# Three rotary units of the sparse attention, moved from the product stage into the stage of the key search's scores

## The chip, the cores and the metric

The kernel runs on one core of one Trainium2 chip. The metric is the device time of one execution in microseconds, the median of several runs. The engines are TensorE (PE in the profile, PEld for its weight loads), VectorE (DVE), ScalarE (ACT), GpSimd (POOL) and SyncE (SP), which here only issues transfers.

## What is computed

Two models run one after the other: a block of linear-attention and recurrent mixers with a feed-forward part, and then two hybrid attention layers over 1024 positions of width 1024. The change is in the hybrid layers. What matters of one of them:

```python
h = jnp.einsum('bsd,de->bse', x, w_in)
(dq, dk, dv, sq, sk, sv, iq, ik, iw, fq, fk, fv, ff, gate) = split_columns(h)
...
sq = rope(sq.reshape(B, S, DSA_HEADS, DSA_DIM), pos)      # 4 heads of 64
sk = rope(sk, pos)                                        # one key head
iq = rope(iq.reshape(B, S, IDX_HEADS, IDX_DIM), pos)      # 8 heads of 64
ik = rope(ik, pos)
bo = dsa_attention(sq, sk, sv, iq, ik, iw * IDX_WEIGHT_SCALE, pos, topk)   # topk = 256
...
# in dsa_attention, per block of 128 queries
sc = jnp.einsum('bqhd,bsd->bqhs', qib, ki)
idx_score = jnp.einsum('bqhs,bqh->bqs', jax.nn.relu(sc), wib)
_, idx = lax.top_k(jnp.where(causal[None], idx_score, -jnp.inf), topk)
s = jnp.einsum('bqhd,bqkd->bhqk', qb, kk[idx]) * scale    # attention over the chosen keys
```

So `iq`, `ik` and `iw` are needed for the search of the keys, `sq` and `sk` only in the attention behind it.

## The kernel before, in words

A hybrid layer is the body of a loop of two turns. It is a sequence of stages; in each, all engines run their own list of instructions, held together by semaphores, and a stage begins when all have finished the one before. The matrix XT (the layer's input, transposed, and its rounding rest REST) lies in SBUF. Every product with it is made of three: high by high, high by rest, rest by high (`three_products`, lines 344 to 346). A rotary unit is 128 output features over 1024 positions: `unit_products` issues 2 halves of 512 positions x 8 slices of the contraction x 3 = 48 products of 128x512 into one pair of PSUM banks; there are four pairs. GpSimd splits the unit's weights into high part and rest (lines 451 and 453, or 2039 and 2041), VectorE multiplies the pair by cosine and by sine (lines 472 and 475, or 2121 and 2124), ScalarE's queue issues four transfers that swap the halves of 32 partitions (`turn_halves`, line 372), and VectorE adds the swapped half (line 466, or 2110).

The stages that matter, in this order:

1. The product stage ("pa", `product_stage`): eight rotary units, three for the sparse attention (SQ: four query heads in two, the key head in one) and five for the search (IQ), each in pair u % 4; then a wide product of 332 columns for all eight blocks of 128 positions, one PSUM bank each. Its first use of each pair waits for `scaled`, the second rotation product of the unit that lay there. ScalarE rounds SQ to SQ_high (line 439) and GpSimd subtracts it (line 457, SQ_rest).
2. The score stage (`index_stage`): 8 blocks of queries (t) times 8 heads (h), 64 rows j of 128 queries by 128(t+1) keys. TensorE computes two heads in a step, as products of 64 rows each in fp32 (line 1866), so there are 32 steps; ScalarE takes the relu (line 1878) into one of four slots, VectorE adds it, weighted, to the block's scores (line 1891), and per block takes the greatest (line 1898) and adds the causal mask (line 1899). PSUM pairs are used as j % 4. SyncE loads a few parameters for the attention.
3. The search stage (`search_stage`, "tk"): VectorE and ScalarE find the 256th greatest score of each query in 32 rounds of bisection (ScalarE counts in three blocks, line 1930, VectorE in three, line 1961, and joins them in lines 1965, 1966 and 1958), then VectorE writes the mask. Beside it TensorE computes 20 units (12 that ScalarE copies out, 8 rotary ones) and a wide product of 512 columns. From the 17th unit on it needs pairs that VectorE must free, which does so only behind the search.
4. The sparse attention, which reads SQ_high, SQ_rest and the mask, and the stages behind it.

Of the kernel before, what the change touches and what calls it, by code (L numbers as in the profile page):

```python
# [16 lines left out]
P = 128  # L17
# [357 lines left out]
def product_stage(kit, tag, XT, rest, items, ropes, rope, place, rot, partner, halves, wide):  # L375
# [9 lines left out]
    (products, taken, dve_own, scaled, rope_in, split, rounded, bank_done, wide_taken, high_done, low_done) = (  # L385
        kit.sem(f"{tag}_{n}") for n in ("products", "taken", "dve_own", "scaled", "rope_in", "split", "rounded",
                                        "bank_done", "wide_taken", "high_done", "low_done"))
    with ExitStack() as mem:
# [5 lines left out]
        with nc.Block() as block:  # L394
# [10 lines left out]
            def _(pe):  # L405
# [23 lines left out]
            def _(act):  # L429
                for n in range(U + 1):  # L430
# [14 lines left out]
            def _(pool):  # L445
                for i, (_, width) in enumerate(items):
# [1393 lines left out]
def index_stage(kit, IQ, VS, IS, AM, causal, prepare):  # L1840
# [3 lines left out]
    scored, bent, added, done, own_d = (kit.sem(f"ix_{n}") for n in ("scored", "bent", "added", "done", "own_d"))  # L1844
    H = 8
    SLOTS = 4
    with ExitStack() as mem:
        R = sbuf(nc, mem, "ix_R", [P, SLOTS, S])
        with nc.Block() as block:
            @block.sync  # L1850
            def _(sp):
                prepare.load(sp)

            @block.tensor
            def _(pe):
                for t in range(NT):
                    n = P * (t + 1)
                    for h in range(0, H, 2):
                        j = t * H + h
                        if j >= SLOTS:  # L1860
                            pe.wait_ge(bent, j + 1 - SLOTS + 1)
                        for c in range(0, n, HALF):
                            e = min(n, c + HALF)
                            for m in range(2):
# [3 lines left out]
                                if e == n:  # L1868
                                    last.then_inc(scored, 1)
# [1171 lines left out]
```

## Time and profile before

| | |
|---|---|
| median of 3 runs | 3120.19 us (3117.55 to 3122.45) |
| the profiled execution | 3115.68 us, its span 3114.0 us |
| mean granted TensorE clock | 0.964 |
| busy share: PE, PEld, DVE, ACT, POOL | 91%, 74%, 54%, 32%, 25% |
| product stage, score stage, search stage of layer 0, from us | 1356.8, 1473.8, 1539.2 |

Times in the views are microseconds from the span's start. Products are pipelined: each of 128x512 is recorded with 0.39 us, though one starts every 0.23 us, so a busy PE in a stretch says that it had work, not how much more would fit. A granted clock of 1 is 2.4 GHz, one of 0.5 is 1.2 GHz.

### The profile page before, as it was taken

How to read it: one execution, taken by the hardware profiler on the slowest of the kernel's cores; microseconds unless marked ns; L12 is line 12 of the kernel's file. 1: busy time of each engine (PE TensorE's matmuls, PEld its weight loads, DVE VectorE, ACT ScalarE, POOL GpSimd, SP SyncE). 2: the span in 40 equal slices, each digit the busy share in tenths (PEclk: the TensorE clock that was granted, in tenths of full speed). 3: DMA queues.
4: the chain of work that ended last, by engine and by line, in shares of the span. 5: the costliest groups of instructions: out<-in, count | busy, mean ns of one | idle time of the engine just before them, and what ended most of it. 6: DMA issues, size and time to landing. Idle time of an engine off the chain costs nothing. (4 is left out here: it accounts for less than half of the span.)

```text
span 3114.0 us, 39179 instructions
## 1 busy us (share of the span) xinstructions
PE 2840.1 (91%) x14936; PEld 2311.2 (74%) x14936; DVE 1677.7 (54%) x2806; ACT 983.8 (32%) x1911; POOL 791.7 (25%) x510
## 2 busy tenths in 40 slices
PE   6999888989999999989699889989897898999988
PEld 4768678778888888868388778777684686778767
DVE  5170476534223233333999545675446998265855
ACT  3150454220000000111564034563105560244751
POOL 2233103223233333323033261003130332340021
PEclk9999899999999999999999999999899999999999
DMA  3101002111111111131122420004320224300032
GB/s 113 35 34 49 1 1 99 48 41 38 51 58 38 50 59 48 55 122 47 41 89 89 139 92 1 1 13 165 131 64 3 96 87 123 141 1 1 1 135 95
DMA packets 83146, 194.07 MB, mean 62 GB/s; under 512 B 15488, under 2 KB 34448, under 8 KB 81936
## 3 DMA queue, kind: packets, MB, share of 16 engines
q1 hardware_dynamic: 71056, 153.78, 14.6%
q10 hardware_dynamic: 11904, 37.76, 3.9%
q8 instruction: 123, 2.02, 0.3%
q14 instruction: 63, 0.52, 0.1%
HBM read 141.18 MB, written 33.55 MB: 56 GB/s over the span
## 5 line engine op out<-in xcount | busy, mean ns | idle before, releaser
L344 PE MATMUL psum<-H,tk_W 128*128 128x512 f32 x640 | 250.9, 392 | 23.1 <-DVE OM L2124 22.9
L344 PE MATMUL psum<-H,ffn_W 128*128 128x512 f32 x672 | 262.9, 391 | 4.8 <-DVEq L1716 3.1
L346 PE MATMUL psum<-H,ffn_W 128*128 128x512 f32 x672 | 262.4, 390 | 0.0
L345 PE MATMUL psum<-H,ffn_W 128*128 128x512 f32 x672 | 262.4, 390 | 0.0
L345 PE MATMUL psum<-H,tk_W 128*128 128x512 f32 x640 | 250.3, 391 | 0.0
L346 PE MATMUL psum<-H,tk_W 128*128 128x512 f32 x640 | 250.0, 391 | 0.0
L1930 ACT ACTIVATE MB<-OM,tk_mid 128x384 bf16<-128x384 f32 (+2 forms) x192 | 157.2, 819 | 120.7 <-DVE tk_mid L1958 119.9
L1961 DVE TENSOR_SCALAR_CACHE_REDUCE MB<-OM,tk_mid 128x512 bf16<-128x512 f32 (+2 forms) x192 | 184.3, 1010 | 2.3
L1483 POOL CAST ffn_W<-ffn_W 128x1024 fp32r<-128x1024 f32 (+1 forms) x77 | 65.1, 845 | 471.4 <-PE psum L346 469.6
L2039 POOL CAST tk_W<-tk_W 128x1024 fp32r<-128x1024 f32 (+1 forms) x56 | 53.6, 958 | 512.1 <-PE psum L346 361.0
L1697 DVE TENSOR_SCALAR ffn_Y<-ffn_G,ffn_par 128x1024 f32<-128x1024 f32 x21 | 21.1, 1004 | 288.6 <-ACT ffn_G L1670 288.6
L1670 ACT ACTIVATE ffn_G<-psum 128x1024 f32<-128x1024 f32 x21 | 21.6, 1029 | 445.6 <-PE psum L346 445.6
L344 PEld LDWEIGHTS psum<-H,tk_W 128*128 128x128 f32 x640 | 121.0, 189 | 50.1 <-issue 23.7
L1485 POOL TENSOR_TENSOR ffn_W<-ffn_W,ffn_W 128x1024 fp32r<-128x1024 f32 (+1 forms) x77 | 152.6, 1982 | 6.2
L344 PEld LDWEIGHTS psum<-H,ffn_W 128*128 128x128 f32 x672 | 126.8, 189 | 32.3 <-POOLq L1556 3.5
L346 PEld LDWEIGHTS psum<-H,ffn_W 128*128 128x128 f32 x672 | 126.7, 189 | 26.7
L345 PEld LDWEIGHTS psum<-H,ffn_W 128*128 128x128 f32 x672 | 126.8, 189 | 26.1
L2715 POOL TENSOR_TENSOR fin_W_rest<-fin_W 128x2048 fp32r<-128x2048 f32 x4 | 22.4, 5604 | 462.8 <-ACT fin_W L2685 462.8
L346 PEld LDWEIGHTS psum<-H,tk_W 128*128 128x128 f32 x640 | 121.0, 189 | 25.4
L345 PEld LDWEIGHTS psum<-H,tk_W 128*128 128x128 f32 x640 | 121.0, 189 | 25.3
L344 PE MATMUL psum<-ffn_W,ffn_PR 128*128 128x512 f32 x336 | 131.1, 390 | 0.0
L346 PE MATMUL psum<-ffn_W,ffn_PR 128*128 128x512 f32 x336 | 130.8, 389 | 0.0
(442 smaller groups left out, 7219.7 us busy)
## 6 DMA issues: line engine op xcount, KB each, us to landing
tk_W<-in_w_feat SPq DMA_DIRECT2D x40, 512.0 KB, 3.6
ffn_W<-in_ffn_w_gate SPq DMA_DIRECT2D x21, 512.0 KB, 3.5
ffn_W<-in_ffn_w_val SPq DMA_DIRECT2D x21, 512.0 KB, 3.5
ffn_W<-in_ffn_w_down SPq DMA_DIRECT2D x42, 256.0 KB, 2.6
OM<-in_w_feat SPq DMA_DIRECT2D x16, 512.0 KB, 7.7
OM<-MB ACTq DMA_DIRECT2D x64, 128.0 KB, 2.4
GATE<-OM ACTq DMA_DIRECT2D x16, 512.0 KB, 2.9
OM<-OM ACTq DMA_DIRECT2D x64, 128.0 KB, 2.9
```

Of the source, the lines that this page charges most:

```text
L344: pe.matmul(out, a1, b1, start=start, stop=False)
L345: pe.matmul(out, a1, b2, start=False, stop=False)
L346: return pe.matmul(out, a2, b1, start=False, stop=stop)
L1483: pool.tensor_copy(w1, w).then_inc(self.rounded, 1)
L1485: pool.tensor_tensor(w2, w, w1.bitcast(FP32), ALU.subtract).then_inc(self.split, 1)
L1670: act.activation(G[:, j % 2, 2:2 + S], kit.pair(j % 2), ACT.Copy).then_inc(gate_out, 1)
L1697: own.then(dve.tensor_scalar(y, x[:, 2:2 + S], par[:, 2, j:j + 1], par[:, 3, j:j + 1], ALU.mult, ALU.add))
L1930: last = act.activation(self.MB[:, self.keys(t)], self.IS[:, self.keys(t)], ACT.Sign, scale=-1.0, bias=self.mid[:, 3 + n:4 + n], accum_out ...
L1961: own(dve.tensor_scalar(MB[:, self.keys(t)], IS[:, self.keys(t)], mid[:, n:n + 1], 0.0, ALU.is_lt, ALU.add, accum_out=self.cnt[:, n:n + 1]))
L2039: pool.tensor_copy(w1, w).then_inc(rounded, 1)
L2715: pool.tensor_tensor(w_part(W2, c, 0), w_part(W, c, 0), w_part(W1, c, 0).bitcast(FP32), ALU.subtract).then_inc(w_low_pool, 1)
```

## The change

The three units of the sparse attention leave the product stage, which keeps the five of the search. The score stage loads their weights and the rotation table, splits them on GpSimd, and computes their products in 48 chunks of three (one slice of the contraction of one half), a few behind each step, in proportion to the step's keys and none in the last four steps. The scores use three PSUM pairs; all three units use the fourth, one after the other. The number of chunks issued up to each step is `upto`. VectorE rotates unit u behind the second row of the step `last_step[u]`, in which the unit's last chunk is issued (steps 15, 22 and 27); ScalarE issues the swap four rows later, and VectorE adds the partner another four rows later. The rounding of SQ to its high part and rest goes to the search stage, both on GpSimd, behind its fourth to sixth weights.

```diff
-def product_stage(kit, tag, XT, rest, items, ropes, rope, place, rot, partner, halves, wide):
+def product_stage(kit, tag, XT, rest, items, ropes, rope, place, rot, partner, wide):
...
-                            pe.wait_ge(scaled, U - n_pairs + t // 2 + 1)
+                            pe.wait_ge(scaled, [u for u in range(U) if u % n_pairs == t // 2][-1] + 1)
...
-                    if 0 < n <= len(halves):
-                        plain, high, _ = halves[n - 1]
-                        act.wait_ge(taken, n)
-                        act.activation(high, plain, ACT.Copy).then_inc(high_done, 1)
...
-                    if 0 <= i - 3 < len(halves):
-                        plain, high, low = halves[i - 3]
-                        pool.wait_ge(high_done, i - 2)
-                        pool.tensor_tensor(low, plain, high.bitcast(FP32), ALU.subtract).then_inc(low_done, 1)
...
-def index_stage(kit, IQ, VS, IS, AM, causal, prepare):
+def index_stage(kit, IQ, VS, IS, AM, causal, prepare, XT, rest, items, ropes, rope, table, rot, partner):
...
+    H, SLOTS, PAIRS, PARTS, UNIT_PAIR, CHUNKS = 8, 4, 3, 2, 3, 2 * KT
+    U, STEPS = len(ropes), NT * H // 2
...
+    share = [j // 4 + 1 for j in range(STEPS - 4)]
+    upto = [min(CHUNKS * U, CHUNKS * U * sum(share[:j + 1]) // sum(share)) for j in range(STEPS)]
+    last_step = [[j for j in range(STEPS) if upto[j] >= CHUNKS * (u + 1)][0] for u in range(U)]
...
+                for i, (src, _) in enumerate(items):
+                    if i >= PARTS:
+                        sp.wait_ge(split, i - PARTS + 1)
+                    sp.dma_start(W[:, i % PARTS, :], src).then_inc(w_in[i % PARTS], 16)
+                    if i == 0:
+                        sp.dma_start(table, rope).then_inc(rope_in, 16)
                 prepare.load(sp)
...
+                for i in range(U):
+                    w, w1, w2 = (a[:, i % PARTS, :] for a in (W, W1, W2))
+                    pool.wait_ge(w_in[i % PARTS], 16 * (i // PARTS + 1))
+                    if i >= PARTS:
+                        pool.wait_ge(products, i - PARTS + 1)
+                    pool.tensor_copy(w1, w).then_inc(rounded, 1)
+                    pool.wait_ge(rounded, i + 1)
+                    pool.tensor_tensor(w2, w, w1.bitcast(FP32), ALU.subtract).then_inc(split, 1)
...
+                def chunk(n):
+                    u, c, k = n // CHUNKS, n % CHUNKS // KT, n % KT
+                    if n % CHUNKS == 0:
+                        pe.wait_ge(split, u + 1)
+                        if u:
+                            pe.wait_ge(scaled, u)
+                    w1, w2 = (a[:, u % PARTS, k * P:(k + 1) * P] for a in (W1, W2))
+                    at = slice(c * HALF, (c + 1) * HALF)
+                    last = three_products(pe, kit.pair(UNIT_PAIR)[:, at], w1, w2, XT[:, k, at], rest[:, k, at],
+                                          k == 0, k == KT - 1)
+                    if n % CHUNKS == CHUNKS - 1:
+                        last.then_inc(products, 1)
+
+                def scores(step):
+                    t, h = step * 2 // H, step * 2 % H
+                    n, j = P * (t + 1), 2 * step
+                    if j + 1 >= PAIRS:
+                        pe.wait_ge(bent, j + 1 - PAIRS + 1)
...
+                for step in range(STEPS):
+                    scores(step)
+                    for n in range(upto[step - 1] if step else 0, upto[step]):
+                        chunk(n)
...
+                    for u in range(U):
+                        if j == 2 * last_step[u] + 1 + SLOTS:
+                            act.wait_ge(scaled, u + 1)
+                            if u:
+                                act.wait_ge(turned, u)
+                            turn_halves(act, partner, rot, swapped)
...
+                def rotate(u):
+                    dst, scale = ropes[u]
+                    out = kit.pair(UNIT_PAIR)
+                    dve.wait_ge(products, u + 1)
+                    if u == 0:
+                        dve.wait_ge(rope_in, 16)
+                    else:
+                        dve.wait_ge(swapped, 64 * u)
+                    own(dve.scalar_tensor_tensor(dst, out, scale, cos, ALU.mult, ALU.mult))
+                    dve.scalar_tensor_tensor(rot, out, scale, sin, ALU.mult, ALU.mult).then_inc(scaled, 1)
+
+                def add_partner(u):
+                    dst = ropes[u][0]
+                    dve.wait_ge(swapped, 64 * (u + 1))
+                    own.wait()
+                    dve.tensor_tensor(dst, dst, partner, ALU.add).then_inc(turned, 1)
...
+                        for u in range(U):
+                            if j == 2 * last_step[u] + 1:
+                                rotate(u)
+                            if j == min(2 * last_step[u] + 1 + 2 * SLOTS, NT * H - 1):
+                                add_partner(u)
...
                     pool.tensor_tensor(w2, w, w1.bitcast(FP32), ALU.subtract).then_inc(split, 1)
+                    if 0 <= i - 3 < len(halves):
+                        plain, high, low = halves[i - 3]
+                        pool.tensor_copy(high, plain).then_inc(high_done, 1)
+                        pool.wait_ge(high_done, i - 2)
+                        pool.tensor_tensor(low, plain, high.bitcast(FP32), ALU.subtract).then_inc(low_done, 1)
...
-    items = [(w_feat[m], S) for m in range(8)]
-    items += rows_of(w_tok, 0, 332)
-    dst = [SQ[:, j, :] for j in range(3)] + [IQ[:, j, :] for j in range(5)]
-    ropes = [(dst[m], QK_SCALE if m < 2 else IDX_SCALE if 3 <= m < 7 else 1.0) for m in range(8)]
+    items = [(w_feat[3 + m], S) for m in range(5)] + rows_of(w_tok, 0, 332)
+    ropes = [(IQ[:, m, :], IDX_SCALE if m < 4 else 1.0) for m in range(5)]
...
-    index_stage(kit, IQ, VS, IS, AM, causal, prepare)
+    index_stage(kit, IQ, VS, IS, AM, causal, prepare, XT, REST, [(w_feat[m], S) for m in range(3)],
+                [(SQ[:, m, :], QK_SCALE if m < 2 else 1.0) for m in range(3)], rope, MB[:, 0:4 * S].bitcast(FP32),
+                flat[:, 5 * S:6 * S], flat[:, 6 * S:7 * S])
```

## Rows read from the trace of the kernel before

**Rows 1.** The page: busy time of each engine and its share.
```profile
PE 2840.1 (91%) x14936; PEld 2311.2 (74%) x14936; DVE 1677.7 (54%) x2806; ACT 983.8 (32%) x1911; POOL 791.7 (25%) x510
```

**Rows 2.** Stretches of layer 0: length, busy per engine, granted clock, DMA share, GB/s.
```profile
1356.80:1443.80 87.00, 86.97 (x384) 72.01 (x385) 29.28 (x20) 3.18 (x3) 32.60 (x19) 1.00 0.32 91
...
1473.80:1539.20 65.40, 40.32 (x192) 16.40 (x192) 57.70 (x80) 40.95 (x64) 0.00 (x0) 0.91 0.01 3
```

**Rows 3.** The page: products of the search stage, both layers.
```profile
L344 PE MATMUL psum<-H,tk_W 128*128 128x512 f32 x640 | 250.9, 392 | 23.1 <-DVE OM L2124 22.9
```

**Rows 4.** Timeline, VectorE, product stage: start, length, operation, idle before.
```profile
1379.00 1.23 DVE L472 SCALAR_TENSOR_TENSOR SQ<-psum,pa_table 128x1024 f32<-128x1024 f32 x1 [8.51 <-PE psum L346]
...
1381.27 2.38 DVE L466 TENSOR_TENSOR SQ<-SQ,OM 128x1024 f32<-128x1024 f32 x1
...
1444.21 1.22 DVE L472 SCALAR_TENSOR_TENSOR IQ<-psum,pa_table 128x1024 f32<-128x1024 f32 x1 [7.39 <-PE psum L346]
...
1446.48 1.22 DVE L466 TENSOR_TENSOR IQ<-IQ,OM 128x1024 f32<-128x1024 f32 x1
```

**Rows 5.** Timeline, all engines, start of the product stage.
```profile
1349.70 0.36 SPq L400 DMA_DIRECT2D OM<-in_w_feat  x1
...
1353.32 1.04 POOL L451 CAST pa_W<-OM 128x1024 fp32r<-128x1024 f32 x1 [57.76 <-DMA OM<-in_w_feat]
...
1356.83 0.50 PE L344 MATMUL psum<-H,pa_W 128*128 128x512 f32 x1 [0.96 <-POOL pa_W L453]
```

**Rows 6.** Timeline, PE, score stage: one step of 512 and one of 896 keys.
```profile
1488.59 1.13 PE L1866 MATMUL psum<-IQ 64*128 64x512 f32 x4 [0.42 <-ACT ix_R L1878]
...
1515.65 1.77 PE L1866 MATMUL psum<-IQ 64*128 64x512 f32 x8 [0.47 <-ACT ix_R L1878]
```

**Rows 7.** Timeline, PE, sparse attention: into and out of 64-row products.
```profile
1881.70 0.50 PE L2139 MATMUL psum<-SQ_high 64*128 64x512 f32 x2
...
1882.04 0.40 PE L2139 MATMUL psum<-SQ_rest,SQ_high 64*128 64x512 f32 x2
...
1882.85 0.34 PE L2139 MATMUL psum<-SQ_high,SQ_rest 64*128 64x384 f32 x2
...
1883.12 0.93 PE L2224 MATMUL psum<-MB,identb 128*128 128x512 bf16 x4
```

**Rows 8.** Timeline, VectorE, score stage.
```profile
1490.71 5.89 DVE L1891 SCALAR_TENSOR_TENSOR OM<-ix_R,VS,OM 128x512 f32<-128x512 f32 x7
...
1516.61 8.69 DVE L1891 SCALAR_TENSOR_TENSOR OM<-ix_R,VS,OM 128x896 f32<-128x896 f32 x7
...
1525.33 1.09 DVE L1898 TENSOR_REDUCE AM<-OM 128x1 f32<-128x896 f32 x1
...
1538.41 0.29 DVE L1899 TENSOR_TENSOR OM<-OM,CONST 128x128 f32<-128x128 f32 x1
```

**Rows 9.** Timeline, ScalarE and its queue, product and score stage.
```profile
1392.19 2.44 ACTq L372 DMA_DIRECT2D OM<-MB  x4
...
1516.60 0.92 ACT L1878 ACTIVATE ix_R<-psum 128x896 f32<-128x896 f32 x1 [0.99 <-DVE OM L1894]
```

**Rows 10.** Stretch of the search stage behind PE's wait, columns as in rows 2.
```profile
1732.00:1736.00 4.00, 4.00 (x11) 3.13 (x11) 1.90 (x3) 0.00 (x0) 0.00 (x0) 0.57 0.73 164
```

**Rows 11.** Timeline, VectorE, search stage: rounds of the bisection, and its end.
```profile
1541.76 0.22 DVE L1958 TENSOR_SCALAR tk_mid<-tk_lo,tk_steps 128x6 f32<-128x6 f32 x1
...
1576.80 0.17 DVE L1965 TENSOR_TENSOR tk_keep<-tk_cnt,tk_need 128x6 f32<-128x6 f32 x1
...
1580.52 0.17 DVE L1965 TENSOR_TENSOR tk_keep<-tk_cnt,tk_need 128x6 f32<-128x6 f32 x1
...
1580.73 2.37 DVE L1966 SCALAR_TENSOR_TENSOR tk_lo<-tk_keep,tk_steps,tk_lo 128x6 f32<-128x6 f32 x1
...
1684.52 0.17 DVE L1967 TENSOR_SCALAR tk_mid<-tk_lo 128x6 f32<-128x6 f32 x1
```

**Rows 12.** Timeline, GpSimd, search stage.
```profile
1580.69 2.39 POOL L2041 TENSOR_TENSOR tk_W<-tk_W 128x1024 fp32r<-128x1024 f32 x1
```

More of the change, by code:

```diff
@@ L384, in product_stage @@
     swapped = [kit.sem(f"{tag}_swapped{n}") for n in range(turns)]
-    (products, taken, dve_own, scaled, rope_in, split, rounded, bank_done, wide_taken, high_done, low_done) = (
+    products, taken, dve_own, scaled, rope_in, split, rounded, bank_done, wide_taken = (
         kit.sem(f"{tag}_{n}") for n in ("products", "taken", "dve_own", "scaled", "rope_in", "split", "rounded",
-                                        "bank_done", "wide_taken", "high_done", "low_done"))
+                                        "bank_done", "wide_taken"))
     with ExitStack() as mem:
@@ L1854, in _ @@
             @block.tensor
             def _(pe):
[L1856 to L1864, printed above, removed]
-                                rows = slice(64 * m, 64 * m + 64)
-                                last = pe.matmul(kit.pair((j + m) % SLOTS)[:, c:e], IQ[rows, h // 2, t * P:(t + 1) * P],
-                                                 IQ[rows, 4, c:e], start=True, stop=True)
-                                if e == n:
-                                    last.then_inc(scored, 1)
+                def chunk(n):
[10 more added lines that the diff above has]
+                        last.then_inc(products, 1)
@@ new lines, in scores @@
+                def scores(step):
[3 more added lines that the diff above has]
+                        pe.wait_ge(bent, j + 1 - PAIRS + 1)
+                    for c in range(0, n, HALF):
+                        e = min(n, c + HALF)
+                        for m in range(2):
+                            rows = slice(64 * m, 64 * m + 64)
+                            last = pe.matmul(kit.pair((j + m) % PAIRS)[:, c:e], IQ[rows, h // 2, t * P:(t + 1) * P],
+                                             IQ[rows, 4, c:e], start=True, stop=True)
+                            if e == n:
+                                last.then_inc(scored, 1)
@@ L1877, in _ @@
                         act.wait_ge(added, j - SLOTS + 1)
[L1878 removed]
+                    act.activation(R[:, j % SLOTS, 0:n], kit.pair(j % PAIRS)[:, 0:n], ACT.Relu).then_inc(bent, 1)
+                    for u in range(U):
[4 more added lines that the diff above has]
+                            turn_halves(act, partner, rot, swapped)
             @block.vector
@@ L1996, in select, with search_stage @@
             own.then(dve.tensor_scalar(MB[:, self.keys(t)], A[:, 0:n], 1.0, -NEG, ALU.subtract, ALU.mult))
-def search_stage(kit, XT, rest, items, topk, staged, partner, rot, fox, GATE, FQD, rope, DQD, DV):
+def search_stage(kit, XT, rest, items, topk, staged, partner, rot, halves, fox, GATE, FQD, rope, DQD, DV):
     nc = kit.nc
@@ L2893, in layer @@
         items += rows_of(w_tok, 332, 844)
-        search_stage(kit, XT, REST, items, topk, staged, slots_of(0, 2), slots_of(2, 4), [QK_SCALE] * 2 + [1.0] * 2, GATE, FQD, rope, DQD, DV)
+        search_stage(kit, XT, REST, items, topk, staged, slots_of(0, 2), slots_of(2, 4),
+                     [(SQ[:, m, :], SQ_high[:, m, :], SQ_rest[:, m, :]) for m in range(3)], [QK_SCALE] * 2 + [1.0] * 2, GATE, FQD, rope, DQD, DV)
     gates = ExitStack()
```

21 lines of the change are left out of this document (13 added, 8 removed).

## The prediction, made before the change was run

> **What bounds the kernel now.** I read the page's engine totals first: TensorE is busy 91% of the span [rows 1], so the question is where it is not. The stretches of layer 0 answer that [rows 2]. The eight rotary units of the product stage (1356.8 to 1443.8) keep PE at 86.97 of 87.00 us, and its wide half starts without a gap behind them: what leaves them is worth its full price. In the stage of the key search's scores, 1473.8 to 1539.2, PE is busy 40.32 of 65.40 us and VectorE 57.70. VectorE's rows there run without a gap, 5.89 us for seven accumulations of 512 keys, 8.69 us for seven of 896 [rows 8], and PE waits for ScalarE, which waits for VectorE: VectorE bounds this stage. Last comes the search stage behind it. Its page row [rows 3] has PE idle 22.9 us before the first product of a unit, released by VectorE's rotation at L2124: once in each layer, some 11.5 us, PE has all four PSUM pairs full while VectorE is still searching. So in that stage VectorE sets the time until PE starts again, and what delays VectorE before that point is paid in full.
>
> **Part 1: three units leave the product stage.** Rotations of consecutive units begin 10.87 us apart (1379.00 to 1444.21 is six units) [rows 4]; with 48 products a unit, one product is 0.2265 us. Three units: -32.6 us a layer. But the PSUM pair order changes. With five units the wide half's first tile lies in the pair of unit 4, the unit just finished, so PE waits for its rotation, whose two operations take 2.27 us by their starts [rows 4], 2.5 with the signals. Before, the last unit's pair was the fourth to be used, behind the products of six tiles, which hid it. Sum: -30.1 us a layer. ScalarE's three roundings and GpSimd's three remainders leave at no gain, as PE had no gap there.
>
> **Part 2: the same 144 products, in the score stage.** Count from PE's first score product (0).
>
> *Start.* The weights are loaded by this stage's own block. At the product stage's start, load issue to GpSimd's cast is 3.6 us (1349.70 to 1353.32) and the split is in use 3.5 us after that (1356.83) [rows 5]. So chunk 0, which stands behind step 2 (the whole-number rule gives 0, 0, 1 chunks up to steps 0, 1, 2), starts at 7.2. PE would otherwise be there after some 2 us, and all later scores stand behind the chunk: VectorE runs dry for some 5 us. The parameter loads now wait behind the third weight load; nobody needs them until the attention.
>
> *PE's chain from there to chunk 47.* 48 chunks of three products are 32.6 us. Scores: a step of 512 keys takes 1.13 us and one of 896 keys 1.77 [rows 6], so 0.213 us per 128 keys and 0.28 us of start and end; steps 3 to 27 have 109 such units, 23.2 us. New are the changes between 64-row fp32 pairs and 128-row products, which the stage does not show. The nearest rows are those of the sparse attention [rows 7]: entering 64-row products the second pair starts 0.34 us after the first, where a 512-column product takes 0.23; leaving them, the next starts 0.27 us after one of 384 columns, which takes 0.17. Add a late first start of some 0.1 us: I take 0.3 us a step for both changes, 24 steps, 7.2 us. Bounds: nothing, and 0.6 (the 0.28 exposed twice). The Trainium skill, "TensorEngine Tiling (Array Packing)", Key Properties, says that changing the tiling mode drains TensorE. By that rule each step also pays the drain, which makes the 0.3 more likely than nothing.
>
> *Two stalls.* All three units share one pair. Step 15 issues chunks 15 and 16 (floor of 48x40/112 is 17), step 22 chunks 31 and 32 (floor of 48x78/112 is 33): the first chunk of the next unit is in the same step as the last of the one before, and waits until that is rotated. VectorE must first take both rows of that step: after the scores, two relus (0.92 each at 896 keys [rows 9], say 0.65 at 512), an add of 0.84 (5.89/7 [rows 8]), then 2.3 of rotation, less the 0.7 of the chunk that runs meanwhile: 4.4 us with signals, about the same at 768 keys. Queued behind PE's wait are all further scores, so ScalarE and then VectorE run dry too. Twice: 8.8 us.
>
> Chain: 7.2 + 32.6 + 23.2 + 7.2 + 8.8 = 79.0 us.
>
> *Tail.* The last two rows before the third rotation come 2.1 us behind the chunks (two relus of 0.92, two adds of 1.24, beside 2.2 us of chunks), rotation 2.3, then what VectorE did from 1525.33 to 1538.70, 13.4 us [rows 8], and one add of the partner, 1.2 [rows 4]: 19.0. The stage: 98.0. The four swap issues on ScalarE's queue (2.44 us [rows 9]) fall thrice: in the last case four slots of relus lie ahead of VectorE, in the two others PE sets the pace and ScalarE catches up in a few rows. I take them at nothing; uncovered they cost 2.4 each.
>
> *Clock.* After its wait in the search stage, in which it did nothing, PE restarts at the 1.2 GHz level: the granted clock is 0.57 from 1732 to 1736 [rows 10], full before and soon after. PE's 5 us of idleness at the start of this stage should bring that level too: chunks run 4 us at half speed, 2.0 us. The boundary stalls are shorter and I add nothing for them; if each brings it, another 4.
>
> Stage after: 100.0, before 64.9 (1473.8 to 1538.7): +35.1 us a layer.
>
> *VectorE and GpSimd.* During GpSimd's subtraction of 2.39 us (1580.69) VectorE's L1966, an operation with two SBUF inputs on six columns, lasts 2.37 us [rows 11, 12]. The accumulations here have two SBUF inputs too, and three splits of 3.4 us run beside them: 3.4 of the first two while VectorE is dry anyway, the others while PE is the pace. I take nothing, at most 5. The Trainium skill, "SBUF — State Buffer", Who interferes with whom, says it as a rule: a VectorE instruction with two SBUF inputs and a GpSimd one that reads SBUF lock each other out for a whole instruction. By that rule up to 7 us of VectorE's time would go, most of it inside PE's waits; the trace agrees on the small tiles.
>
> **Part 3: the halves' rounding moves to GpSimd in the search stage.** Behind items 3, 4 and 5 GpSimd gets a cast and a subtraction more, 3.4 us each time, in VectorE's search. A round without GpSimd takes 3.72 us (1576.80 to 1580.52); 32 rounds last 142.7 us (1541.76 to 1684.52) [rows 11] where 119.0 would do: 23.7 us went with 14 splits (two at its start, then one every 10.9 us), 1.7 each. Three more: +5.1 us a layer, and PE's wait of rows 3 grows by it. Bounds: nothing (each falls beside the counting passes, which are not slowed) and 10.3 (each fully exposed). PE's own items are not late: a unit leaves GpSimd 10.9 us and it needs 6.9.
>
> **Sum.** -30.1 + 35.1 + 5.1 = +10.1 us a layer, two layers +20.2. The profiled execution took 3115.7 us; the median of the runs is 3120.2, so 4.5 above it. 3115.7 + 20.2 = 3135.9 against the profile, 3140.4 against the median: I say 3140.
>
> **Rivals.**
> A, VectorE stays the bound and PE fits between: for it, PE's 25 idle us in the stage. The stage would be 64.9 plus three rotations with their adds (3 x 3.5 = 10.5) plus the start's 5, 80.4; -30.1 + 15.5 and 0 to 5 for the search: -10 to -15 a layer, 3091 to 3101. It needs the two pair waits and the changes of shape to cost nothing; it decides from a stage under about 90 us on. Against it: PE's chain with its tail is already 82 us without both (98.0 - 8.8 - 7.2), and its 25 idle us are fewer than the 32.6 put in.
> B, no difference: changes of shape free, no clock loss, search at 0 to 3: the stage 91, -30.1 + 26 + 2 = -2 a layer, with what else varies 3114 to 3126.
> C, the clock: each stall, and the light score steps as well, keep PE at 1.2 GHz for about half of the chunks: +16 a layer, 3172, and with some of the search's upper bound up to 3180. For it, the level fell in this stage already (its mean is 0.91 [rows 2]); against it, it was back within microseconds, and PE will be busier.
>
> **Numbers.** Forecast as summed, 3126 to 3164: 0.60. A 0.14, B 0.13, C 0.13. The time is that of the first. Range: from B's low (all low bounds together give 3112) to 3166 (forecast plus the search fully exposed and a late clock: 3140 + 10 + 16, of which C holds what lies above). A change of 0.2%, 6.2 us, is about what a measurement of this kernel can tell from none. Faster by more: A and a little of B, 0.15; within: most of B, 0.12; slower: 0.73. The forecast's own range is 3126 to 3164.
>
> **What would show it.** The product stage's units 54.4 us instead of 87.0, with a PE gap of 2.5 before the first wide tile released by L475. In the score stage: first chunk 7 us in, released by GpSimd's split; two PE waits of 4 to 5 us released by VectorE's rotation; start-to-start of PE steps at 896 keys about 3.8 us against VectorE's 2.7 (two adds of 1.24 and a quarter of the tile's ends); the stage near 100. In the search stage PE's wait for L2124 16 us a layer instead of 11.5. The prediction is wrong if PE steps of 896 keys keep VectorE's 2.7 us pitch (A), or if the granted clock in the score stage is under 0.9 (C).

## The result, and the profile after

The changed kernel takes **3165.6 us** (median of 4 runs, 3162.0 to 3171.2) against 3118.9 for the kernel before on the same chip: ratio **1.0147**, 95% interval 1.0133 to 1.0161. I had said 3140. The sign is right, the size is not: +46.7 us instead of +20, and 3165.6 lies outside the forecast's own 3126 to 3164.

The page of the changed kernel, TensorE's line and the row that answers to [rows 3]:

```profile
PE 2876.8 (91%) x14936; PEld 2324.2 (74%) x14936; DVE 1680.6 (53%) x2806; ACT 972.6 (31%) x1905; POOL 794.7 (25%) x516
L344 PE MATMUL psum<-H,tk_W 128*128 128x512 f32 x640 | 251.6, 393 | 29.6 <-DVE OM L2196 28.3
```

PE's busy time grew by some 37 us (from 2840.1) although the number of products is the same. The last kernel below has the same 14936 products, hardly any of them at a lower clock, and 2855.7 us: so more than half of the growth is not the new order of the products; I take it for the clock. L2196 is the search stage's second rotation product, L2124 before; PE waits 28.3 us for it instead of 22.9.

The stretches of the score stage after, all engines (length, busy time and count of PE, PEld, DVE, ACT, POOL; granted clock; DMA share; GB/s), and last the whole stage:

```profile
1446.00:1450.00 4.00, 1.48 (x12) 0.93 (x12) 2.04 (x6) 1.38 (x7) 0.00 (x0) 0.96 0.66 213
1450.00:1454.00 4.00, 0.00 (x0) 0.00 (x0) 0.00 (x0) 0.00 (x0) 2.95 (x2) 0.50 0.76 311
1454.00:1462.00 8.00, 7.16 (x20) 3.98 (x21) 3.25 (x7) 1.77 (x6) 3.83 (x3) 0.50 0.32 84
1462.00:1470.00 8.00, 8.00 (x27) 3.52 (x26) 4.11 (x10) 2.19 (x6) 0.00 (x0) 0.70 0.01 2
...
1486.00:1490.00 4.00, 1.18 (x3) 0.83 (x3) 3.56 (x5) 0.00 (x0) 2.67 (x1) 0.66 0.00 0
1490.00:1494.00 4.00, 4.00 (x13) 2.19 (x12) 0.35 (x1) 1.09 (x2) 0.00 (x0) 0.50 0.00 0
1494.00:1514.00 20.00, 19.55 (x92) 11.50 (x90) 13.19 (x17) 8.66 (x13) 0.00 (x0) 1.00 0.12 27
1514.00:1518.00 4.00, 0.61 (x3) 0.49 (x3) 3.25 (x3) 0.00 (x0) 0.00 (x0) 1.00 0.00 0
1518.00:1522.00 4.00, 4.00 (x13) 1.78 (x12) 0.00 (x0) 0.59 (x1) 0.00 (x0) 0.58 0.00 0
1522.00:1540.00 18.00, 18.00 (x79) 10.53 (x79) 12.50 (x13) 7.85 (x10) 0.00 (x0) 1.00 0.13 31
...
1446.35:1557.84 111.49, 85.87 (x337) 45.12 (x337) 69.26 (x90) 38.20 (x64) 10.78 (x6) 0.87 0.14 40
```

Three holes in PE's column (1450, 1486, 1514), and behind each a stretch in which PE is fully busy at the lower of its two levels. After the first it lasts past 1462. Elsewhere the clock is full, and PE, no longer VectorE, is the engine without gaps up to its last chunk. Over the whole stage the granted clock is 0.87; it was 0.91 before [rows 2].

PE's own rows after: the end of the units and the wide half, the start of the score stage, the first change of unit, steps of 640 and 896 keys, and the wide half of layer 1 (start, busy time, instruction, idle time before it):

```profile
1412.00 0.39 PE L346 MATMUL psum<-H,pa_W 128*128 128x512 f32 x1
1414.93 0.39 PE L344 MATMUL psum<-pa_W,H 128*128 128x332 f32 x1 [2.54 <-DVE MB L467]
...
1415.92 0.48 PE L346 MATMUL psum<-pa_W,H 128*128 128x332 f32 x1
1416.19 0.48 PE L344 MATMUL psum<-pa_W,H 128*128 128x332 f32 x1
...
1446.35 0.49 PE L1899 MATMUL psum<-IQ 64*128 64x128 f32 x4 [0.79 <-PEq L394]
...
1454.47 0.79 PE L344 MATMUL psum<-H,ix_W 128*128 128x512 f32 x1 [5.96 <-POOL ix_W L1873]
1455.07 0.63 PE L345 MATMUL psum<-H,ix_W 128*128 128x512 f32 x1
...
1484.05 0.40 PE L346 MATMUL psum<-H,ix_W 128*128 128x512 f32 x1
1488.82 0.77 PE L344 MATMUL psum<-H,ix_W 128*128 128x512 f32 x1 [4.37 <-DVE OM L1937]
1489.39 0.63 PE L345 MATMUL psum<-H,ix_W 128*128 128x512 f32 x1
...
1494.97 1.35 PE L1899 MATMUL psum<-IQ 64*128 64x512 f32 x8
...
1497.84 1.35 PE L1899 MATMUL psum<-IQ 64*128 64x512 f32 x8
...
1531.21 0.39 PE L346 MATMUL psum<-H,ix_W 128*128 128x512 f32 x1
1531.53 1.77 PE L1899 MATMUL psum<-IQ 64*128 64x512 f32 x8
1533.23 0.50 PE L344 MATMUL psum<-H,ix_W 128*128 128x512 f32 x1
1533.57 0.40 PE L345 MATMUL psum<-H,ix_W 128*128 128x512 f32 x1
...
1535.50 1.77 PE L1899 MATMUL psum<-IQ 64*128 64x512 f32 x8
...
2324.26 0.39 PE L344 MATMUL psum<-pa_W,H 128*128 128x332 f32 x1 [2.54 <-DVE MB L467]
...
2325.57 0.31 PE L346 MATMUL psum<-pa_W,H 128*128 128x332 f32 x1
2325.72 0.31 PE L344 MATMUL psum<-pa_W,H 128*128 128x332 f32 x1
```

The wide half starts 2.93 us after the last unit's last product. Its first four products still come at full rate, then for a dozen one of 332 columns comes every 0.28 us instead of every 0.15. In layer 1 the gap is the same and the products behind it stay at 0.15. Chunk 0 starts 8.12 us into the stage. The unit change waits 4.37 us for the second rotation product (L1937). A step of 896 keys with three chunks repeats every 3.97 us.

VectorE's rows after show who waits for whom (L1953 accumulates, L1936 and L1937 rotate, L1943 adds the partner):

```profile
1447.56 2.19 DVE L1953 SCALAR_TENSOR_TENSOR OM<-ix_R,VS,OM 128x128 f32<-128x128 f32 x5
1457.19 1.65 DVE L1953 SCALAR_TENSOR_TENSOR OM<-ix_R,VS,OM 128x128 f32<-128x128 f32 x2 [7.45 <-ACT ix_R L1916]
...
1486.33 1.21 DVE L1936 SCALAR_TENSOR_TENSOR SQ<-psum,MB 128x1024 f32<-128x1024 f32 x1
1487.47 1.21 DVE L1937 SCALAR_TENSOR_TENSOR OM<-psum,MB 128x1024 f32<-128x1024 f32 x1
...
1493.65 0.55 DVE L1956 TENSOR_SCALAR OM<-ix_R,VS 128x640 f32<-128x640 f32 x1 [4.05 <-ACT ix_R L1916]
...
1545.03 9.63 DVE L1953 SCALAR_TENSOR_TENSOR OM<-ix_R,VS,OM 128x1024 f32<-128x1024 f32 x7
1554.57 1.22 DVE L1943 TENSOR_TENSOR SQ<-SQ,OM 128x1024 f32<-128x1024 f32 x1
1555.71 1.21 DVE L1965 TENSOR_REDUCE AM<-OM 128x1 f32<-128x1024 f32 x1
```

**The ledger of layer 0**, start to start. Product stage, first product to first score: 117.0 before (1356.83 to 1473.79), 88.7 after (1357.68 to 1446.35): -28.3, forecast -30.1. Score stage: 65.5 before, 111.5 after (to 1557.8): +46.0, forecast +35.1. Search stage, to the attention's start: 282.4 and 287.5: +5.1, forecast +5.1. Sum +22.8 where I had 10.1: 10.9 of the 12.7 us missed are in the score stage. In layer 1 the three stages moved by -29.9, +45.2 and +2.9, together +18.2, so 8.1 are missed there. The stretch from layer 0's attention to layer 1's product stage, which no edit touches, took from 416.5 to 423.6 us in the twelve traces, and a few of the 46.7 us lie in it (3.4 between these two traces). The terms below are those of layer 0.

That stage splits at two products, chunk 0's first and chunk 47's last: start 8.1, **chain** 84.9, tail 18.4. My terms were 7.2, then 71.8 (79.0 without its start) with 2.0 for the clock, then 19.0. The experiments are read by the same three figures; they are figures of one execution each, and some of them differ by chance (see the table at the end of the experiments).

### The profile page after: what moved, and what is told of

It is laid out like the page before. It is cut to its first block and busy times, and to the rows that moved or that the text cites. A ratio compares the mean times of both kernels' runs of the same rounds, so it can differ in the third digit from the quotient of the medians.

```text
span 3160.4 us, 39197 instructions
## 1 busy us (share of the span) xinstructions
PE 2876.8 (91%) x14936; PEld 2324.2 (74%) x14936; DVE 1680.6 (53%) x2806; ACT 972.6 (31%) x1905; POOL 794.7 (25%) x516
## 5 line engine op out<-in xcount | busy, mean ns | idle before, releaser
L344 PE MATMUL psum<-H,tk_W 128*128 128x512 f32 x640 | 251.6, 393 | 29.6 <-DVE OM L2196 28.3
L1953 DVE SCALAR_TENSOR_TENSOR OM<-ix_R,VS,OM 128x128 f32<-128x128 f32 (+7 forms) x112 | 94.4, 843 | 70.0 <-ACT ix_R L1916 62.1
L344 PE MATMUL psum<-ffn_W,ffn_PR 128*128 128x512 f32 x336 | 131.1, 390 | 0.0
```

The lines of the kernel that those rows point to most:

```text
L344: pe.matmul(out, a1, b1, start=start, stop=False)
L1953: ins = dve.scalar_tensor_tensor(out, R[:, j % SLOTS, 0:n], VS[:, t, 64 + h:65 + h], out, ALU.mult, ALU.add)
```

## The experiments

I had two theories. **The clock**: each wait of PE also brings a stretch at 1.2 GHz, at the start and behind both unit changes. **Changes of shape and work that cannot overlap**: PE's list is simply longer than I summed.

### PE kept busy during its waits

```diff
+                    if n == 0:
+                        spin(kit, pe, UNIT_PAIR, 6)
+                    elif n % CHUNKS == 0:
+                        j = 2 * last_step[u - 1]
+                        pe.wait_ge(bent, j)
+                        spin(kit, pe, (j + 2) % PAIRS, 4)
                     if n % CHUNKS == 0:
                         pe.wait_ge(split, u + 1)
```

This kernel adds products of constants in PE's three waits; nothing reads them.

> The changed kernel with products of constants put into the three waits of PE in the score stage: six ahead of the first chunk, four at each of the two changes of unit (behind them PE still waits for the same semaphores). The waits stay as long as they are; only the clock can change. Theory 1, the clock: the two waits for the rotation and the wait for the split each bring the 1.2 GHz level, and what PE does after them at half speed costs about 6 + 2.5 + 2.5 us a layer, so the granted clock of the stage goes to about 1.0 and the kernel gets 18 to 22 us faster, 3144 to 3148. Theory 2, the occupancy: PE is over-full by its products and the changes of shape alone, and the low clock falls where VectorE would be waiting anyway: at most 5 us faster, 3160 or more.

Measured: 3146.0 us, ratio 1.0091 (1.0074 to 1.0108), kernel before 3117.6 on that chip, within the first theory's range. Windows of this kernel (columns as above):

```profile
1450.00:1454.00 4.00, 4.00 (x10) 1.71 (x9) 0.37 (x2) 0.00 (x0) 2.09 (x2) 1.00 0.94 383
1454.00:1462.00 8.00, 6.87 (x32) 3.43 (x32) 4.41 (x8) 2.62 (x8) 4.74 (x3) 1.00 0.32 88
...
1486.00:1490.00 4.00, 4.00 (x24) 2.48 (x21) 1.44 (x2) 1.68 (x3) 0.00 (x0) 1.00 0.00 0
```

The waits are as long as before (chunk 0 starts 8.3 us in), but the clock stays full (0.98 over the stage). The chain is 76.2 instead of 84.9, and the score stage is 8.6 us shorter in layer 0 and 8.5 in layer 1. Work that nobody needs took some 17 us off the changed kernel. That the clock costs this much is shown; what is left of the excess, with a full clock, is the second theory's part.

### The unit-change waits taken away

```diff
+    for u in range(1, U):
+        first = [j for j in range(STEPS) if upto[j] >= CHUNKS * u][0]
+        upto[first] = upto[first + 1] = CHUNKS * u
```

No chunk of the next unit is issued in the step that ends a unit, nor in the one behind it.

> The changed kernel, but the first chunk of the second and third unit is held back for two steps behind the last chunk of the one before (the held chunks follow in one step). PE then has two score steps to do while VectorE rotates. Theory 1: the two waits (8.2 us a layer) go and with them the slow stretch behind them (some 5 us): 20 to 26 us faster, 3140 to 3146. Theory 2: the waits go, the clock changes nothing, and the larger batch that follows starves VectorE for part of it: 8 to 16 us faster, 3150 to 3158.

Measured: 3143.6 us, ratio 1.0085 (1.0068 to 1.0102), again as the first theory had it. The chain is 74.4: 10.5 us less than in the changed kernel. There the two waits were 4.37 and 3.85, or 8.2 (I had 8.8), so more than the waits went: the stretches at half speed behind them too. The plan has a price of its own, some 2 us: the steps without chunks wait 0.79 to 0.96 us for ScalarE and VectorE. The clock at the start is untouched here.

### No chunks in the first eight steps

```diff
-    share = [j // 4 + 1 for j in range(STEPS - 4)]
+    share = [j // 4 + 1 if j >= 8 else 0 for j in range(STEPS - 4)]
```

> The changed kernel with the chunks spread over steps 8 to 27 instead of 2 to 27, so that the weights have arrived and are split when the first chunk comes up. The two changes of unit stay. Theory 1: the wait at the start (6 us) and the slow stretch behind it (6 us) go, a layer: 20 to 24 us faster, 3142 to 3146. Theory 2: the first two blocks then go at VectorE's pace, not PE's, and PE's chunks are as many as before and pile up later: 8 to 12 us faster, 3154 to 3158.

Measured: 3157.1 us, ratio 1.0126 (1.0109 to 1.0143): a miss of the first theory's number. The start's wait is gone, yet the ratio fell only from 1.0147, some 7 us. PE's rows of this kernel say why:

```profile
1451.04 0.49 PE L1899 MATMUL psum<-IQ 64*128 64x128 f32 x4 [0.36 <-ACT ix_R L1916]
1451.89 1.22 PE L1899 MATMUL psum<-IQ 64*128 64x256 f32 x4 [0.36 <-ACT ix_R L1916]
```

and so do two of its windows:

```profile
1455.00:1465.00 10.00, 8.36 (x22) 3.67 (x22) 9.20 (x11) 3.89 (x10) 5.46 (x3) 0.50 0.29 82
...
1490.00:1500.00 10.00, 9.98 (x35) 6.27 (x36) 2.48 (x3) 2.60 (x4) 0.00 (x0) 0.70 0.02 6
```

PE had no long wait here, only the light 64-row scores of the first blocks, with gaps of 0.36 us for ScalarE, and the clock fell to 1.2 GHz all the same: the first step of 256 keys takes 1.22 us (0.70 in the kernel whose PE was kept busy). (The kernel before does this too, its clock is 0.66 from 1475 to 1480; there VectorE, which bounds the stage, has no gap in that time.) The chunks behind began cold, were more in a step, and the two changes of unit waited longer (4.74 and 4.54 us). My reason for the saving was wrong: not the wait alone drops the clock. That early chunks would have held it up is only half true: in the kernels below that issue chunk 0 without a wait, the clock stays full over these steps in layer 0 and falls even so in layer 1.

### Part 3 alone, on the kernel before

```diff
-                  halves=[(SQ[:, m, :], SQ_high[:, m, :], SQ_rest[:, m, :]) for m in range(3)], wide=wide)
+                  halves=[], wide=wide)
...
+                    if 0 <= i - 3 < len(halves):
+                        plain, high, low = halves[i - 3]
+                        pool.tensor_copy(high, plain).then_inc(high_done, 1)
+                        pool.wait_ge(high_done, i - 2)
+                        pool.tensor_tensor(low, plain, high.bitcast(FP32), ALU.subtract).then_inc(low_done, 1)
```

> The kernel before with one part of the change alone: the rounding of SQ to its high part and rest is done in the search stage, on GpSimd, behind items 3 to 5. By the prediction's term: VectorE's search ends 5.1 us later a layer (between 0 and 10.3), PE's wait for L2124 grows from 22.9 to about 33 us over both layers, and the kernel is 10 us slower, 3129. Rival: the search's rounds take it up beside their counting passes, and the kernel is within 4 us of before; the 28.3 us that the changed kernel shows for that wait lie between the two.

Measured: 3128.9 us, ratio 1.0035 (1.0023 to 1.0048), or +11.3 us. Its page row answers to [rows 3]:

```profile
L344 PE MATMUL psum<-H,tk_W 128*128 128x512 f32 x640 | 251.0, 392 | 29.6 <-DVE OM L2129 28.3
```

The wait rose from 22.9 to 28.3, the very number of the changed kernel, and not to the 33 that I expected. By the traces the 32 rounds of the bisection take 4.2 us more in layer 0 and 2.9 in layer 1, PE's wait grows by 3.3 and 2.1, and the search stage by 3.8 and 3.3. The product stage kept its 117.0 us, so the roundings that left it brought nothing, as forecast. This part of the change alone makes the kernel slower.

### The wide half begins with free pairs

```diff
-                    for t in range(NT):
+                    for t in ([2, 3, 4, 5, 6, 7, 0, 1] if k == 0 else range(NT)):
```

> The changed kernel with one thing different in the product stage: the first slice of the wide product takes the tiles in the order 2 to 7, 0, 1, so that the pair of the unit just finished is the last to be used. Theory 1: PE's wait of 2.5 us at the change from the units to the wide half goes, and with it the slow stretch that followed it (products every 0.28 us instead of 0.15), together 3 to 4 us a layer: 6 to 8 us faster than the changed kernel, 3158 to 3160. Rival: the slow stretch came from something else than the wait, and only 2.5 us a layer come back, 3161; or the low level is only moved to the start of the score stage, and nothing changes.

Measured: 3159.7 us, ratio 1.0122 (1.0105 to 1.0139), on another chip, with the kernel before at 3123.5. The product stage of layer 0, to the first score, falls from 88.7 to 84.3 us: -4.3, the gap of 2.7 and the 1.6 that the wide products lost at half speed behind it. In layer 1 it falls by 2.8, the gap alone. So a gap of 2.5 us can bring a cold stretch, but need not: five of the traced kernels have it in both layers, and of these ten wide halves seven ran partly at half rate and three did not.

The score stage has the changed kernel's program here, yet its chain is 82.4 instead of 84.9: the steps of 256 keys behind chunk 0 took 2.74, 1.92, 1.52 and 1.53 us, where those of the changed kernel took 2.73, 2.74, 2.73 and 2.14 (1.53 at a full clock). How long the low level lasts is not fixed by the program, and a single trace's price of it carries some 2.5 us of chance.

### Both cures for the score stage

The held-back plan of the second experiment with the start's products of constants (as in the first, but none at the unit changes).

```diff
+        upto[first] = upto[first + 1] = CHUNKS * u
...
+                    if n == 0:
+                        spin(kit, pe, UNIT_PAIR, 6)
```

> The changed kernel with the six products of constants ahead of the first chunk (as in e1, there alone) and the held-back chunks of e2. If the two are the separate costs that theory 1 has, their gains add: e2's 22 us and some 10 to 12 for the slow stretch at the start, 3131 to 3134, and the granted clock of the score stage is about 1.0. If they share a cause (PE's occupancy as a whole), less: 3138 or more.

Measured: 3135.7 us, ratio 1.0042 (1.0028 to 1.0057), just above the first range on a chip that is some 6 us slower with the kernel before (3123.5 against 3117.6). The chain is 69.3. Against the 74.4 of the plan alone, the clock at the start is worth 5.1 us in layer 0; in layer 1 it is 3.0.

What the changed kernel's chain holds can now be added up step by step, from one start to the next. At a full clock and without waits its steps come to 67.0 us (32.6 + 23.2 + 24 x 0.44 makes 66.4; the rest is step 3, which has no chunk behind it and waits for ScalarE). The waits take 8.5: 4.54 and 4.00 from start to start. At half rate it loses 5.2 at the start, 2.5 behind the first change of unit and 1.7 behind the second. Together 84.9. The products of constants, which took away the clock's part alone, gave back 8.7 of these 9.4.

### Chunks grouped behind every second step

The kernel of the last experiment, its products of constants at the start included, with the pair order, with the halves' rounding moved behind the search's 20th to 22nd weights, and with a step's chunks held until the next odd step, which halves the changes of shape.

```diff
+    upto = [upto[j] if j % 2 or j >= STEPS - 4 else upto[max(j - 1, 0)] for j in range(STEPS)]
...
-                    if 0 <= i - 3 < len(halves):
+                    if 0 <= i - 19 < len(halves):
```

> e6 and three more edits: chunks are issued behind every second step in double batches (half of the changes between the two shapes of product), the tile order of e5, and the halves' rounding put behind items 19 to 21 of the search stage, where VectorE's search is over. Priced one by one: the changes of shape at 0.44 us a step, 12 steps less, 5 us a layer; the order 3 to 4; the halves 5.6. Together 28 us less than e6: 3103 to 3107, below the kernel before. Rival to the first price: VectorE is the bound once the waits are gone, so fewer changes of shape give nothing and double batches starve it: 3115 or more.

Measured: 3131.3 us, ratio 1.0032 (1.0022 to 1.0041), a clear miss, and what the rival had said (3115 or more). Two of the edits did their part: the product stage kept its -4.3, and PE's wait for the rotation fell to 24.1 us. The grouping did not: the chain grew from 69.3 to 73.2. In this kernel two score steps follow each other without chunks between:

```profile
1517.16 1.77 PE L1905 MATMUL psum<-IQ 64*128 64x512 f32 x8
1519.94 1.77 PE L1905 MATMUL psum<-IQ 64*128 64x512 f32 x8 [1.00 <-ACT ix_R L1922]
```

With three pairs for the scores, the second step waits 1.00 us for ScalarE's relu, more than the 0.44 that it saves; and behind four of the double batches of layer 0 VectorE is idle for 1.7 to 5.0 us. The chunks had been hiding ScalarE.

### The weights loaded and split a stage earlier

The held-back plan, the pair order and the late halves, no grouping and no products of constants. The first two units' weights are loaded and split in the product stage, into slots that had held the weights of its own units.

```diff
+                    if i == slots:
+                        for n in range(2):
+                            ahead.load(sp, n)
...
+                    if U - 2 <= i < U:
+                        ahead.part(pool, i - U + 2)
```

> The held-back chunks of e2, the order of e5 and the late halves of e7, without products of constants and without double batches; the weights of the first two units are loaded and split in the product stage already (four slots for its own weights instead of six), those of the third at the start of the score stage. The first chunk has nothing to wait for: the 6 us of idle PE a layer go, and with them the slow stretch, where e6 takes only the latter: e6's 3132, less 12 for the idle time, less 8 and 11 for order and halves: 3098 to 3104. Rival: the stage is bound elsewhere by then and the start is worth nothing more than e6 has: 3110 to 3115.

Measured: **3114.4 us, ratio 0.9969** (0.9959 to 0.9979), faster than the kernel before (3123.5), but in the rival's range of 3110 to 3115 and not in mine. Chunk 0 starts 2.1 us in, the chain is 70.9, the stage 91.4. In layer 1 the chain is 74.9: there the low level came at the stage's start although chunk 0 did not have to wait (0.50 from 2330 to 2335), and in both layers it came again in the batch of five chunks, behind two waits of 0.79 and 0.96 us.

### The chunks of the held-back steps spread

```diff
+    share = [j // 4 + 1 if j not in (15, 22) else 0 for j in range(STEPS - 4)]
+    upto = []
+    for a, z in ((0, 16), (16, 23), (23, STEPS)):
+        part = share[a:z]
+        upto += [CHUNKS * (a > 0) + CHUNKS * (a > 16) + CHUNKS * sum(part[:j + 1]) // sum(part) for j in range(z - a)]
```

> The kernel of e8_ahead with another plan of the chunks: the batches of five and seven chunks behind the two held-back steps are spread, so that no step issues more than four; everything else is the same. Theory 1: the batches starve VectorE, which is idle 3.07 and 2.91 us behind them in layer 0 of e8_ahead and does not get this back; spreading returns 2 to 3 us a layer, so the kernel comes out 4 to 6 us below e8_ahead. Theory 2: TensorE's chain sets the end of the score stage wherever its chunks lie, and VectorE's idleness only moves: within 2 us of e8_ahead, and the score stage again near 90.9 us.

The kernel of the last experiment ran once more beside it, unchanged:

> The kernel of e8_ahead once more, beside e9_smooth on the same chip, with more rounds. If e8_ahead's ratio of 0.9969 stands, this is 0.996 to 0.998 of the kernel before, 6 to 12 us below it; if that was an accident of one chip, the interval takes in 1.

Measured, side by side on one chip with the kernel before at 3124.2: the smooth plan takes **3109.3 us, ratio 0.9955** (0.9942 to 0.9968); the kernel of the last experiment, run again, 3113.2, ratio 0.9967 (0.9958 to 0.9976). So the first gain stands. The medians differ by 3.9 us, at the edge of the first theory's 4 to 6, but the intervals overlap, and beside the repeated kernel's trace the score stage is only 1.2 us shorter in each layer, 2.3 in all, near the second theory's 2. Which of the two holds stays open. Windows of the smooth plan, layer 0 and then layer 1, and the third score step of layer 1:

```profile
1455.00:1470.00 15.00, 14.32 (x58) 6.97 (x58) 10.35 (x16) 6.67 (x14) 2.18 (x2) 1.00 0.00 0
1470.00:1480.00 10.00, 9.99 (x53) 6.11 (x49) 8.99 (x12) 3.91 (x6) 1.71 (x1) 1.00 0.24 54
1480.00:1500.00 20.00, 19.11 (x90) 11.51 (x87) 16.35 (x19) 9.11 (x12) 0.00 (x0) 1.00 0.12 27
...
2321.00:2326.00 5.00, 3.71 (x19) 2.37 (x19) 2.04 (x6) 1.64 (x7) 0.00 (x0) 0.74 0.69 225
2326.00:2330.00 4.00, 3.64 (x15) 1.84 (x11) 2.12 (x6) 1.10 (x4) 0.00 (x0) 0.50 0.45 147
2330.00:2335.00 5.00, 5.00 (x25) 2.36 (x21) 2.83 (x6) 1.98 (x6) 0.00 (x0) 0.97 0.01 3
...
2323.28 0.70 PE L1917 MATMUL psum<-IQ 64*128 64x128 f32 x4 [0.36 <-ACT ix_R L1934]
```

In layer 0 there is no hole, the clock is full, the chain is 68.3 and the stage 88.7. Its ledger: product stage to first score 84.3 (-32.6), score stage +23.2, search +1.8. In layer 1 PE has no wait of 1 us either, yet the level falls in the third score step and costs 2.6 us: chain 70.9, stage 91.5. Light steps with gaps of 0.33 and 0.36 us can bring it, here as in the late start above; in layer 0 the same steps did not.

Start, chain and stage of all kernels with the new score stage, from TensorE's rows; the tail is 18.3 to 18.4 us throughout, 18.9 with the late start:

| kernel | start, layer 0 | chain | stage | start, layer 1 | chain | stage |
|---|---|---|---|---|---|---|
| changed | 8.1 | 84.9 | 111.5 | 8.0 | 84.2 | 110.6 |
| pair order (same score stage) | 7.8 | 82.4 | 108.6 | 8.6 | 82.5 | 109.5 |
| PE kept busy | 8.3 | 76.2 | 102.9 | 7.5 | 76.2 | 102.1 |
| held-back plan | 8.3 | 74.4 | 101.1 | 8.3 | 72.6 | 99.3 |
| no chunks in eight steps | 12.2 | 78.6 | 109.7 | 14.3 | 76.2 | 109.4 |
| both | 8.2 | 69.3 | 96.0 | 8.6 | 69.6 | 96.7 |
| grouped | 8.6 | 73.2 | 100.1 | 10.9 | 73.6 | 102.7 |
| weights ahead | 2.1 | 70.9 | 91.4 | 2.4 | 74.9 | 95.8 |
| weights ahead, again | 2.1 | 69.3 | 89.8 | 2.3 | 72.0 | 92.7 |
| smooth plan | 2.1 | 68.3 | 88.7 | 2.3 | 70.9 | 91.5 |

The two runs of one program, weights ahead, differ by 1.6 us in layer 0 and 3.1 in layer 1. In layer 0 all of it is the batch of five chunks behind the wait of 0.96 us: 7.49 us long in one run, its first nine products coming every 0.43 us, and 5.88 in the other, where behind the same wait they come every 0.23.

## Why the prediction was right in kind and short in size

**What bounds the kernel** held: PE took over the score stage from VectorE, as its pitch of 3.97 us at 896 keys shows, where VectorE needs 2.7. Rival A (VectorE stays the bound) and rival B (no difference) fell by that. I had put the pitch at about 3.8.

**Part 1**, -30.1 forecast, -28.3 measured. The five units take 54.5 us (54.4 forecast), the gap 2.7 beyond a product's own time (2.5). What I left out is 1.6 us of the wide half at half speed behind it; in layer 1, where that stretch did not come, the stage gave 29.9.

**Start**: 7.2 forecast, 8.1 measured. The weight's landing took 4.5 us from its issue, not the 3.6 of [rows 5]; why stays open, as other loads were issued behind it there too.

**Products and scores**, 32.6 + 23.2: taken over unchanged, and the 67.0 us that the chain's steps need at a full clock bear them out, together with the changes of shape. I had left out step 3, which waits for ScalarE with no chunk behind it: +0.6.

**Changes of shape**: I took 0.30 us a step from [rows 7]; they cost 0.44. A step of 896 keys is 1.49 (seven units of 0.213) + 2.04 (nine products) + 0.44 = 3.97, one of 640 keys is 1.07 + 1.36 + 0.44 = 2.87. The rows say where: the score starts 0.32 us after the last chunk product instead of 0.23, the next chunk's first product 1.70 after the score instead of 1.49, and the second 0.34 instead of 0.23. I had taken some 0.1 for each of the three joints; the middle one, out of the scores, is twice that. Over 24 steps +3.4 us. The Trainium skill, "TensorEngine Tiling (Array Packing)", Key Properties, says that a change of tiling mode drains TensorE. The trace agrees in that each change costs time, 0.44 us a step; the price is only in the rows.

**Two stalls**: 8.8 forecast; 8.2 of idle time, 8.5 from start to start, released as forecast.

**Tail**: 19.0 forecast, 18.4 measured, up to the search's first operation; the partner's add and VectorE's last block are as in [rows 4] and [rows 8].

**Swap issues and the lock of VectorE and GpSimd**: nothing forecast, and little found. VectorE's accumulations did lengthen under a split: the pair at 1484.22, beside a cast and a subtraction of GpSimd from 1484.59 on, took 2.19 us instead of 1.61, just before the first rotation. That delays the rotation for which PE waits, and fits the first wait being the longer one, 4.37 us against 3.85.

**Part 3**: +5.1 a layer forecast. The search stage grew by 5.1 and 2.9 us in the two layers, and the part alone brought +11.3 us for the kernel (7 to 15 by its interval). The 5.1 of layer 0 is in part luck: the bisection itself grew by 3.9 and 2.6, so 1.3 and 0.9 for each burst of GpSimd where I had 1.7, and PE's wait rose to 14.2 us a layer instead of 16. The rest of layer 0 lies behind the wait, in a stretch whose length differs by 1.5 us from trace to trace.

**The clock is the step that failed.** I took 2.0 us a layer: "The boundary stalls are shorter and I add nothing for them". Measured in layer 0: 5.2 at the start, 4.2 behind the two unit changes, and 1.6 in the wide half, 11.0 in all. Two errors lie in that term. I read the cold stretch off one row where PE came out of a long idleness into dense work [rows 10], and took it for 4 us; here it came out into light score steps with a chunk each, and ran at 0.50 and then 0.70 for some 12 us (some 6 us in the pair order's trace, where the score stage has the same program). And I took a stall of 4 us for too short, without a row to say so; the rows of the wide half, after only 2.54 us, say that it can come even then. Rival C named the mechanism, stalls and light score steps, and gave 3172; its sign, a granted clock under 0.9 in the score stage, came true with 0.87. Only its size was too high: not half of all chunks ran slow, some six of the 48 did, and the score steps among them. I had given it 0.13.

In sum for layer 0, beyond the forecast: the clock 9.0, the changes of shape 3.4, step 3 0.6, the start 0.9, the gap 0.2, less 0.3 for the stalls and 0.6 for the tail; and 0.6 less because the ledger counts the stage before to the search's first operation (65.5, where I took 64.9). That gives 12.6, against 12.7 in the ledger.

**Why the idea itself can pay.** I had argued that 32.6 us cannot go into PE's 25 idle us, and they do not: the score stage grows by 23.2 even at its best. But the product stage gives 32.6, so 9.4 a layer remain if no hole is made and the clock stays full, as in layer 0 of the smooth plan; in its layer 1 it is 6.6. The change as it stood made four (before the wide half, at the score stage's start, at the two unit changes) and put GpSimd's bursts into the search besides.

## What to carry to other kernels

Price a wait of TensorE twice: its length, and what the work behind it loses at 1.2 GHz. Here holes of 3.8 to 6 us brought 1.7 to 5 us more each, and holes of 2.5 us nothing or 1.6. Take a range and not a number: the same program lost 5.2 us in one trace and 2.5 less in another. Light work can bring the low level without any hole. When work is moved into the gaps of another stage, its inputs have to be ready in the stage before, a shared PSUM pair must be left empty for a step or two at each handover, and the work is spread so that no batch starves the engine that used to be the bound. When two shapes of products alternate, read the whole period of a step, not only its joints, or a third of the change's price is missed.

## What the runs showed of the hardware

- A gap of 2.54 us in PE's work was followed by about a dozen products at half rate (one of 332 columns every 0.28 us instead of 0.15) in seven of ten wide halves, and by none in three.
- One program in two runs: the same wait of 0.96 us, and behind it fifteen products in 5.2 us, at half rate at first, or in 3.6 us at full rate.
- Products of constants in PE's waits kept the granted clock at 0.98 over the score stage instead of 0.87, and took 8.6 us a layer off it.
- Light work alone lets the clock fall: with 64-row products and gaps of 0.36 us, and no long wait, it was at 1.2 GHz by the score stage's fifth step of the late-start kernel (by the third in layer 1 of the smooth plan), and stayed there through the window from 1455 to 1465 in which PE was busy for 8.36 of 10 us.
- Going from 128-row products to 64-row fp32 pairs and back costs 0.44 us a step, of which 0.21 lie between the score's start and the next chunk.
- A VectorE pair of accumulations that met GpSimd's split took 2.19 us instead of 1.61.
- Three more casts and subtractions of GpSimd beside VectorE's 32 rounds of bisection made these longer by 3.9 and 2.6 us in the two layers.
